# Attention scores get their bias on the vector engine instead of through an identity matmul

## The reference

```
scores = einsum('bnqkgd,bnskd->bnkgqs', qb, k_band) * (SWA_HD ** -0.5)
scores = where(mask, scores + alibi, -1e30)
probs  = softmax(concatenate([scores, sink], -1), -1)[..., :-1]
```

## Time and profile before

| | |
|---|---|
| time, median of 3 runs | 2416.94 us (2416.58 to 2419.4) |
| the profiled execution: its own time, its span | 2421.2 us, 2419.2 us |
| TensorE busy | 2307.2 us (95%), granted clock 0.975 of 2.4 GHz over the span |
| VectorE busy | 1420.8 us (59%) |
| ScalarE busy | 1096.6 us (45%) |
| DMA | 346.77 MB, mean 143 GB/s |

### The profile page before, as it was taken

How to read it: one execution, slowest core, us unless ns; L and a number is a source line. 1 busy time by engine, 2 the same in 40 slices (tenths; PEclk the granted TensorE clock), 3 DMA queues, 4 the chain that set the end, 5 groups by cost and what they waited for, 6 DMA issues and landing times.

```text
span 2419.2 us, 36469 instructions
## 1 busy us (share of the span) xinstructions
PE 2307.2 (95%) x14412; PEld 1983.7 (82%) x14412; DVE 1420.8 (59%) x2286; ACT 1096.6 (45%) x1729; POOL 27.3 (1%) x55
## 2 busy tenths in 40 slices
PE   8899799999999889999999999999999989898999
PEld 7689799999999867765478887888887764798999
DVE  4355577777777662337743455666665347566665
ACT  5454344444444365446642334323324556544543
POOL 0000000000000000000000000000000000000000
PEclk9999899999999999989999999999999999999999
DMA  8234576666666433200022324444554301254554
GB/s 281 87 122 132 192 246 233 227 231 220 232 227 231 142 105 122 76 18 18 19 70 94 98 89 142 144 148 165 198 188 146 118 29 34 77 187 140 185 181 140
DMA packets 253822, 346.77 MB, mean 143 GB/s; under 512 B 7138, under 2 KB 217602, under 8 KB 252674
## 3 DMA queue, kind: packets, MB, share of 16 engines
q1 hardware_dynamic: 246354, 315.70, 39.4%
q0 software_dynamic: 7344, 29.36, 3.5%
HBM read 343.95 MB, written 1.08 MB: 143 GB/s over the span
## 4 chain that ended last, share of the span: by engine, by line
PE 89%; DVE 5%; ACT 3%; DMA 1%; issue 1%; SPq 0%; DVEq 0%; ACTq 0%
PE PS L739 22%; PE PS L740 22%; PE PS L741 22%; PE PS L978 7%; PE PS L835 3%; PE PS L851 2%; PE PS L804 2%; PE PS L863 2%; ACT CR L1151 1%; PE PS L1084 1%; PE PS L841 1%; DVE CR L1514 1%; DMA ring<-in_w_gate 1%; PE PS L1070 1%; PE PS L1075 1%
## 5 line engine op out<-in xcount | busy, mean ns | idle before, releaser
L739 PE MATMUL PS<-HH,CR 128*128 128x256 f32 (+1 forms) x2512 | 794.7, 316 | 36.9 <-DVE HL L1553 15.2
L740 PE MATMUL PS<-HL,CR 128*128 128x256 f32 (+1 forms) x2512 | 784.6, 312 | 0.0
L741 PE MATMUL PS<-HH,CR 128*128 128x256 f32 (+1 forms) x2512 | 784.3, 312 | 0.0
L1514 DVE TENSOR_TENSOR CR<-ring,CR 128x1024 fp32r<-128x1024 f32 x328 | 400.2, 1222 | 456.1 <-ACT CR L1151 448.5
L739 PEld LDWEIGHTS PS<-HH,CR 128*128 128x128 f32 x2512 | 486.3, 194 | 71.9 <-issue 39.6
L740 PEld LDWEIGHTS PS<-HL,CR 128*128 128x128 f32 x2512 | 486.6, 194 | 29.4 <-issue 4.6
L741 PEld LDWEIGHTS PS<-HH,CR 128*128 128x128 f32 x2512 | 486.0, 193 | 25.0
L1151 ACT ACTIVATE CR<-ring 128x1024 fp32r<-128x1024 f32 x328 | 343.7, 1050 | 283.7 <-PE PS L741 270.3
L1314 ACT ACTIVATE CR<-ring 128x1024 fp32r<-128x1024 f32 x192 | 202.9, 1059 | 311.4 <-PE PS L741 186.4
L739 PE MATMUL PS<-AR,CR 128*128 128x256 f32 (+1 forms) x960 | 317.7, 331 | 7.3 <-DVE AR L1613 7.3
L1759 DVE TENSOR_TENSOR CR<-ring,CR 128x1024 fp32r<-128x1024 f32 x192 | 234.7, 1224 | 148.2 <-ACT CR L1314 144.1
(11 more groups left out here) (176 smaller groups left out, 2175.0 us busy)
## 6 DMA issues: line engine op xcount, KB each, us to landing
ring<-in_w_in SPq DMA_DIRECT2D x66, 1024.0 KB, 5.2
ring<-in_ffn_w SPq DMA_DIRECT2D x64, 1024.0 KB, 5.5
ring<-in_w_gate SPq DMA_DIRECT2D x32, 1024.0 KB, 5.4
ring<-in_w_up SPq DMA_DIRECT2D x32, 1024.0 KB, 5.3
ring<-in_w_down SPq DMA_DIRECT2D x32, 1024.0 KB, 4.8
BR<-in_w_mod SPq DMA_DIRECT2D x48, 512.0 KB, 6.0
BR<-in_w_mod POOLq DMA_DIRECT2D x48, 512.0 KB, 3.7
ring<-in_w_out SPq DMA_DIRECT2D x12, 1024.0 KB, 5.1
```

Source lines behind the costliest of these rows:

```text
L739: pe.matmul(bank, wh, xh, start=start, stop=False)
L740: pe.matmul(bank, wh, xl, start=False, stop=False)
L741: return pe.matmul(bank, wl, xh, start=False, stop=stop)
L1514: dve.tensor_tensor(lo, src, hi, ALU.subtract).then_inc(lo_done, 1)
```

## The change

TensorE no longer adds the bias; the scores matmul closes its group and signals at once. VectorE adds it with `tensor_tensor_reduce`, which in one pass writes scores plus bias back in place into PSUM and leaves the maximum of the sums, begun from `floor`, in `nm`. In the order it shows as two instructions: `ISA PS,SM<-PS,BR` and a read of the accumulator, `ISA SM`. With a sink, `floor` is the sink. Without one, it is the maximum over the keys that have no bias, found first by a `tensor_reduce` over columns 256 to 511. A last `tensor_scalar` negates. Units without a bias (`x["bias"] is None`) keep the single reduction; all units with a sink have a bias.

```diff
--- before.py
+++ after.py
@@ -831,15 +831,9 @@
                     for u in us:
-                        bank, x = score_bank(u0 + u), units[u]
-                        mm = pe.matmul(bank[:, 0:x["nk"]], x["q"], x["k"], start=True, stop=x["bias"] is None)
-                        if x["bias"] is None:
-                            mm.then_inc(scores_ready, 1)
-                    for u in us:
-                        bank, bias = score_bank(u0 + u), units[u]["bias"]
-                        if bias is not None:
-                            pe.matmul(bank[:, 0:bias.shape[-1]], IDENT, bias, start=False, stop=True
-                                      ).then_inc(scores_ready, 1)
+                        x = units[u]
+                        pe.matmul(score_bank(u0 + u)[:, 0:x["nk"]], x["q"], x["k"], start=True, stop=True
+                                  ).then_inc(scores_ready, 1)
@@ -1575,11 +1569,17 @@
                     dve.wait_ge(scores_ready, g + 1)
-                    if x["sink"] is None:
+                    if x["bias"] is None:
                         dve.tensor_reduce(nm, s, AX.X, ALU.max, negate=True).then_inc(negmax, 1)
                         return
-                    step(dve.tensor_reduce(m, s, AX.X, ALU.max))
-                    dve.tensor_scalar(nm, m, x["sink"], -1.0, ALU.max, ALU.mult).then_inc(negmax, 1)
+                    nb = x["bias"].shape[-1]
+                    floor = x["sink"]
+                    if floor is None:
+                        floor = m
+                        step(dve.tensor_reduce(m, s[:, nb:x["nk"]], AX.X, ALU.max))
+                    step(dve.tensor_tensor_reduce(out=s[:, 0:nb], in0=s[:, 0:nb], in1=x["bias"], scale=1.0, scalar=floor,
+                                                  op0=ALU.add, op1=ALU.max, accum_out=nm))
+                    dve.tensor_scalar(nm, nm, -1.0, None, ALU.mult).then_inc(negmax, 1)
```

## The result

The changed kernel took 2429.33 us (median of 16 runs, 2421.12 to 2434.16), the kernel before 2419.81 us in 16 runs on the same chip: a ratio of 1.0037, interval 1.0029 to 1.0046. It is slower by 9.5 us between the medians, where I had forecast 2 us less and a range that ended at 2421.5. The profiled execution took 2427.51 us, its span is 2425.7 us and its granted clock 0.966.

A forecast was written before the change was run, and what follows sets the result against it. NA was taken as bound by TensorE's work and an equal 4.32 us loop through VectorE, SWA by the loop alone. Terms -4.2 - 2.8 + 2.2 = -4.8, plus the NA clock, gave -2.0: 2414.9 us, range 2409.5 to 2421.5.

The forecast's parts named there:

- NA, steady loops: Six loops in each of two NA stages: 4.50 us for 4.32, 12 x 0.18 = +2.2 us.
- NA, start: First scores to first transposes in each NA stage: 7.1 us for 8.53, a gain of 1.4 each, -2.8.
- NA, clock: After each NA start the clock often rises late: 1.9 us a stage, chance 0.6 in each.
- SWA: Sliding-window stage loses the bias group with nothing added on VectorE: 3.7 at low clock, 5.6 at full, taken as -4.2.
- rival of the dearer pass: New VectorE pass costs more with PSUM operand and result: no gain from 0.51, slower by over 4.8 from 0.61; chance 0.13.
- the pass at half rate: Upper end of the new VectorE pass's price: 0.74 us for 0.47, 48 x 0.27 = +13.0, 2427.9 us.
- the two loops forecast at -1.4 each: Sliding-window loops at the lower clock: 3.6 us for 4.99, a gain of 1.4 each, 2.8 together.
- The last two: Last two sliding-window loops: a gain of 0.1 each if the clock stays low, 0.6 if it rises.
- The start and the two loops with 128 keys: Sliding-window stage: gains of 0.5 at the start and about 1.1 together in the two loops, estimated by halves.
- The tail: End of the sliding-window stage: transposes and values at half clock cost up to 0.9 us.
- The ends of the range: 2409.5: full clock everywhere, pass at 0.42; 2421.5: pass at 0.56, clock term in both NA stages.
- the two slower rivals: Dearer VectorE pass, 2427.9 us at its upper end, chance 0.13; clock falling in NA loops, about 2432, chance 0.06.

The follow-up runs named there:

- e8: Kernel before with both normalisations moved ahead of the next two maxima on VectorE, bias still on TensorE: 2409.1 us, ratio 0.9951 to before.
- e3: Changed kernel plus idle identity products between the first scores and first transposes of each NA stage: 2425.05 us, ratio 1.001 to before.
- e1: Changed kernel with VectorE adding the bias in SWA alone, NA keeping the identity product: 2418.56 us, ratio 0.9988 to before.
- e2: Changed kernel with VectorE adding the bias in NA alone, SWA keeping the identity product: 2427.1 us, ratio 1.0022 to before.
- e11: Kernel before with VectorE's order normalise(u), maxima(u+2), normalise(u+1), maxima(u+3), bias still on TensorE: 2411.02 us, ratio 0.9962 to before.
- e7: Changed kernel with both normalisations moved ahead of the next two maxima on VectorE: 2406.47 us, ratio 0.9939 to before.
- e9: Changed kernel with VectorE's order normalise(u), maxima(u+2), normalise(u+1), maxima(u+3): 2403.27 us, ratio 0.9938 to before.

## Why the prediction was wrong

What was right: the NA loop as a loop of waits through VectorE, TensorE no longer the bound, its idle time ahead of the second transposes put down to VectorE, the longer stretch at 1.2 GHz behind each NA start, and SWA at the lower clock to its end. Wrong were sizes, and nearly all to one side (us, against the kernel before; the measured ones from the two profiled executions; eight of the twelve loops lie wholly at the full clock and show the 0.38 by themselves):

| term | forecast | measured |
|---|---|---|
| NA, steady loops | +2.2 | 12 x 0.38 = +4.6 |
| NA, start | -2.8 | -1.1 and -0.9 = -2.0 |
| NA, clock | +1.9 in one stage or both | what the first two loops of a stage take beyond 0.38 each: 1.8 and 2.3, together +4.2 |
| NA, end of layer 1 | none | -0.6 |
| SWA | -4.2 | -1.5 |
| sum | -2.0 | +4.7 |

**The steps that failed are two terms of the sum, "NA, steady loop" (+2.2, measured +4.6) and "SWA" (-4.2, measured -1.5).** They make 5.1 of the 6.7 us between forecast and stages. The steady loop was forecast at 4.50 us and took 4.70. Half of the missing 0.20 is the pass: 0.47 was taken from a pass between SBUF operands without a column, and from pass to product it is 0.59. With the small product at 0.07 for 0.13 that leaves about 0.05 a unit, 0.10 a loop. The rival of the dearer pass had this mechanism, with 0.51 on the whole as the point from which nothing is gained; in effect the pass costs 0.53 on that scale. Its upper end, the pass at half rate, did not come: 0.49 is not 0.74. The rule of the Trainium skill (Vector Engine (DVE) Microarchitecture Reference, section "Points that are easy to get wrong") speaks of two sources in SBUF and so did not bear on a pass with a source in PSUM; no run here shows it at work. The Trainium skill also has a fixed cost of access for VectorE (Perfetto Trace Analysis, section "Optimizing Scalar/DVE Operations"), about 60 ns in SBUF and about 125 ns in PSUM. The trace agrees in part: the accumulator read is 58 ns longer behind a result in PSUM, but the bare pass only 7, and whether the 58 ns are that cost no run here shows.

The other 0.10 is scores to maximum, 1.16 for 1.06. I read 1.06 off MLA, where four instructions take 1.88 and the first unit is ready after half of them. In NA the same four take 1.13, though each lasts 0.59 to 0.69: the two heads, on 64 rows each, run side by side, and the first unit's scores are there only when the second's are. Fewer rows did not make the first result earlier. One reading of mine was off besides: TensorE and the loop did not bound the 4.32 alike, since TensorE's own work is 4.17 (e8). It changes none of the terms.

**"NA, start"** is the same pass four times over (4.43 us for 4.24), and the first scores and the last wait, 0.1 us later each. In layer 1 the start of before was shorter too, 8.37 for 8.53. **The clock** was right in kind and in size, 1.8 and 2.3 us for 1.9, and came in both stages, to which I had given 0.6 apiece. e3 supports it: with the full clock the first loop loses 1.85 and 1.73 us of its 6.93. I had not foreseen that the clock would rise and fall once more.

**"SWA"** fell short in several places. I took 4.2 though my own sum at the low clock was 3.7. Cut at the second transposes, the two loops forecast at -1.4 each gave 1.30 and 1.29, as they should. The last two, forecast at -0.1 each, lost 0.27 each: from 3.70 I had taken away the full-clock gain and added back 0.52 for the scores only, but the transposes at half clock take 0.62 for 0.37 (122.04 to 122.66), and the two passes 1.30 for 1.20. 3.6 + 0.25 + 0.10 is 3.95, measured 3.97. The start and the two loops with 128 keys gave 0.6 together, for 1.6, an estimate by halves. The tail, from the last second transpose to the next stage, is 1.2 longer (6.61 to 7.80), for "up to 0.9".

The ends of the range do not follow from the terms that are named for them: 2410.5 less 48 x 0.05 is 2408.1 and not 2409.5, and 2415.9 plus 48 x 0.09 is 2420.2 and not 2421.5.

The chances erred too: the two slower rivals were weighed as alternatives, 0.13 and 0.06, while a moderate share of both came together.

**Open.** The stages account for 4.7 us and the spans differ by 6.5, of which 1.7 lie in stages whose code is the same, and the medians differ by 9.5 (7.0 to 11.1 by the interval). So about half of the difference between the medians has no cause shown. The sum of e1 and e2 against before is only about +3. The granted clock over the whole span goes with the time inside one kernel: the changed kernel's fastest run, 2421.12 us, had 0.972, its five slowest 0.966 or 0.967. Whether a later stage sometimes meets the clock worse because the earlier one ended at another time, I did not test.

## What to carry to other kernels

Where an engine shows no gap, add up the waits of the loop as well: if they give the same period, taking work off that engine buys only the part of it that lies on the loop, and whatever the partner gets is paid in full. Here 1.06 us of TensorE's work bought 0.64 and cost 1.03 on VectorE, 0.38 us a loop. Change the order first, and move the work after it: the order alone made the kernel before 8 to 12 us faster (e11, e8), and the stages with a bias, 4.7 us longer by the move in the old order, are 4.2 and 5.9 us shorter by it in the new ones (e7 against e8, e9 against e11). Price an operation from a row with the same memories and the same kind of scalar; here the column and the result in PSUM made 0.06 us each.

## What the runs showed of the hardware

- `tensor_tensor_reduce` over 256 fp32 columns: 425 ns with a constant start and its result in SBUF, 432 into PSUM, 493 with a column; its accumulator read 83 or 141 ns. An in-place add of 256 columns in PSUM took 0.42 to 0.43 us.
- Two heads' fp32 score products on 64 rows each took 1.13 us for four instructions of 512 columns at 2.4 GHz, 96-row ones 1.88; the first maximum started 1.16 us after the start of the former and 1.06 after that of the latter.
- In NA of layer 0 of the changed kernel the granted clock was 1.00 for about 4 us, in which TensorE was busy 2.06 of 4, and then fell to 0.50 for about 4 us, though TensorE was busy 3.98 of 4 in these. In steady loops it stayed at 1.00 with 12.56 us of work in 18. Before and after the change alike it was 0.50 from 1046 to 1064, ahead of this stage, with TensorE shown as busy 17.5 and 17.2 of the 18 us. That the emptier TensorE had delayed it at the start agrees with the Trainium skill (TensorE: Matmul & The Clock Gate, section "What's actually happening"), where activity releases the throttle; e3's early rise (6 us into the stage for 12.5) is the run that shows it. The stretch ahead of the stage is a case in which a TensorE shown as busy stayed at the lower clock.
